# One unused 32-byte tile ahead of the phase tiles of a hybrid decoder layer

## What is computed

```python
h = _rmsnorm(x, norm_g[l])
proj = jnp.einsum('bsd,de->bse', h, w_in[l])             # 2048 -> 5456 columns
xa, ga, q, ckv, gb, qi, ki, wi = jnp.split(proj, IN_SPLITS, axis=-1)
ya = _rglru_branch(xa, ...) * jax.nn.silu(ga)            # conv, two gates of 128x128 blocks, a scan over the tokens
yb = _dsa_branch(q, ckv, qi, ki, wi, ...) * jax.nn.silu(gb)
# _dsa_branch: 16 index heads score every causal key, each query keeps 256 keys,
# 8 heads of attention over the kept latents (256 wide), read-out and value projection
y = jnp.concatenate([ya, yb], axis=-1)
x = x + jnp.einsum('bse,ed->bsd', y, w_out[l])
return _rmsnorm(x, final_norm_g)
```

## Time and profile before

| | |
|---|---|
| median of 3 runs | 1666.22 us (1665.55 to 1667.6) |
| the profiled execution's own time | 1666.16 us |
| its span, first to last instruction | 1664.4 us |
| PE busy | 1611.6 us, 97% |
| PEld busy | 1311.7 us, 79% |
| DVE, ACT, POOL busy | 51%, 35%, 25% |
| granted TensorE clock, mean | 0.994 of full |

### The profile page before, as it was taken

How to read it: one execution, slowest core, us unless ns; L and a number is a source line. 1 busy time by engine, 2 the same in 40 slices (tenths; PEclk the granted TensorE clock), 3 DMA queues, 4 the chain that set the end, 5 groups by cost and what they waited for, 6 DMA issues and landing times.

```text
span 1664.4 us, 21182 instructions
## 1 busy us (share of the span) xinstructions
PE 1611.6 (97%) x7403; PEld 1311.7 (79%) x7403; DVE 856.6 (51%) x1497; ACT 580.3 (35%) x849; POOL 421.7 (25%) x285
## 2 busy tenths in 40 slices
PE   4999999999999999999999999999998899999998
PEld 4678999888888888888888888777776788888886
DVE  7317555577777777865555554377777000031003
ACT  7225555433443343332111111354555122232320
POOL 1112222222222221222222222210010444444550
PEclk8999999999999999999999999999999999999999
DMA  7412111122222122223222221321222532237322
GB/s 258 88 39 67 48 44 38 32 54 60 60 59 61 38 54 66 66 83 95 75 70 70 74 69 57 108 80 63 66 76 87 205 101 89 95 101 285 127 88 101
DMA packets 132301, 141.35 MB, mean 85 GB/s; under 512 B 8510, under 2 KB 103840, under 8 KB 129952
## 3 DMA queue, kind: packets, MB, share of 16 engines
q1 hardware_dynamic: 130720, 136.55, 26.2%
q0 software_dynamic: 1536, 4.20, 0.8%
HBM read 116.08 MB, written 24.64 MB: 85 GB/s over the span
## 4 chain that ended last, share of the span: by engine, by line
PE 84%; issue 8%; DVE 4%; ACT 2%; DMA 1%; DVEq 0%; POOL 0%; SPq 0%; ACTq 0%; POOLq 0%
PE ps L1022 17%; PE ps L1023 17%; PE ps L1024 17%; PE ps L1282 6%; PE ps L1283 6%; PE ps L1284 6%; PE ps L1109 2%; PE ps L1223 2%; PE ps L1111 2%; PE ps L1187 2%; PE ps L1200 1%; PE ps L1307 1%; PE ps L1308 1%; PE ps L1309 1%; DVE ps L1525 1%
## 5 line engine op out<-in xcount | busy, mean ns | idle before, releaser
L1022 PE MATMUL ps<-hT_hi,w_lo 128*128 128x512 f32 (+2 forms) x1376 | 531.0, 386 | 2.0 <-POOL w_lo L642 2.0
L1024 PE MATMUL ps<-hT_hi,w_hi 128*128 128x512 f32 (+2 forms) x1376 | 528.9, 384 | 0.0
L1023 PE MATMUL ps<-hT_lo,w_hi 128*128 128x512 f32 (+2 forms) x1376 | 528.8, 384 | 0.0
L642 POOL TENSOR_TENSOR w_lo<-w_raw,w_hi 128x512 fp32r<-128x512 f32 (+1 forms) x172 | 237.5, 1385 | 803.0 <-ACT w_hi L723 802.9
L1022 PEld LDWEIGHTS ps<-hT_hi,w_lo 128*128 128x128 f32 (+1 forms) x1376 | 257.0, 187 | 56.7 <-issue 3.5
L1023 PEld LDWEIGHTS ps<-hT_lo,w_hi 128*128 128x128 f32 (+1 forms) x1376 | 256.9, 187 | 53.2 <-issue 0.4
L1024 PEld LDWEIGHTS ps<-hT_hi,w_hi 128*128 128x128 f32 (+1 forms) x1376 | 256.8, 187 | 52.4 <-issue 0.2
L723 ACT ACTIVATE w_hi<-w_raw 128x512 fp32r<-128x512 f32 (+1 forms) x172 | 106.4, 627 | 524.1 <-PE ps L1024 502.8
L1282 PE MATMUL ps<-wo_hi,hT_lo 128*128 128x512 f32 x448 | 178.0, 397 | 3.1 <-DVE hT_lo L1550 3.1
L1609 DVE TENSOR_TENSOR res<-ps,res 128x512 f32<-128x512 f32 x32 | 21.8, 690 | 304.7 <-PE ps L1284 253.9
L1283 PE MATMUL ps<-wo_lo,hT_hi 128*128 128x512 f32 x448 | 177.7, 397 | 0.0
(11 more groups left out here) (179 smaller groups left out, 1712.5 us busy)
## 6 DMA issues: line engine op xcount, KB each, us to landing
w_raw<-in_w_in SPq DMA_DIRECT2D x168, 256.0 KB, 2.8
wo_raw<-in_w_out SPq DMA_DIRECT2D x64, 512.0 KB, 3.6
xin<-in_x SPq DMA_DIRECT2D x8, 1024.0 KB, 5.4
res<-in_x SPq DMA_DIRECT2D x8, 1024.0 KB, 9.4
out<-res SPq DMA_DIRECT2D x16, 512.0 KB, 3.9
y_lru_dram<-sg SPq DMA_DIRECT2D x8, 512.0 KB, 2.8
q_dram<-av SPq DMA_DIRECT2D x8, 512.0 KB, 3.7
gate_dram<-rg SPq DMA_DIRECT2D x8, 512.0 KB, 4.3
```

The costliest lines, as they stand in the source:

```text
L642: nc.gpsimd.tensor_tensor(w_lo[:, j, :, 0:n], w_raw[:, j, :, 0:n], w_hi[:, j, :, 0:n].bitcast(F32), ALU.subtract).then_inc(w_lo_s, 1)
L1022: nc.tensor.matmul(o, wlo, hi, start=(kt == 0), stop=False)
L1023: nc.tensor.matmul(o, whi, lo, start=False, stop=False)
L1024: return nc.tensor.matmul(o, whi, hi, start=False, stop=(kt == KT - 1))
```

## The change

One tile of 8 float32 (32 bytes) per partition is allocated behind `sums`, ahead of the first phase tile, in `layer`. Nothing reads or writes it. No instruction, wait or DMA is added, removed or moved. All phase tiles of all phases begin 32 bytes later, at byte 149888, which is a multiple of 64 and of 128; `hT` and the other lasting tiles stay where they are.

```diff
         w_nat = sb("w_nat", [P, QB, IH])
         sums = sb("sums", [P, QB, 3])
+        sb("line_pad", [P, 8])
 
 
         ph = ExitStack()
```

## The result

The changed kernel takes 1640.27 us (median of 4 runs, 1639.44 to 1640.71) against 1666.91 us before (4 runs). The ratio is 0.984 with a 95% interval of 0.983 to 0.986: 26.6 us less. In a later session the same kernel took 1638.54 us (5 runs, 1637.48 to 1638.66) against 1667.39 us, 0.983 (0.981 to 0.984). The forecast was 1631.4 us, its range 1627 to 1647. So the direction and the size of the gain in the main stages were right, and the two measurements lie 8.9 and 7.1 us above the forecast. The rule given for it (multiples of 64 bytes) is not the one that the runs bear out, as the experiments show.

What follows compares the result with a forecast made beforehand. TensorE, busy for 97% of the span, was taken as the bound through its matmul spacing. Gains of 21.7 + 8.9 + 2.3 + 0.4 + 1.2 + 0.3 = 34.8 us took 1666.2 to 1631.4 us; range 1627 to 1647.

Steps and rivals of the forecast that it cites:

- The rule given for it (multiples of 64 bytes): All matmuls: both operands at multiples of 64 bytes give the last output chunk's pace, 226.7 ns instead of 233.3.
- The main terms: 512-column matmuls falling from 233.3 to 226.7 ns: 21.7 us in the projection, 8.9 us in output chunks one to seven.
- (b): Rival: a rhythm between weight loads and moving stream leaves aligned matmuls at 229 to 230 ns; around 1648 us, chance 0.09.
- (c): Rival: the last chunk's operands sharing a tile, or their distance, sets its pace; no gain, 1666 us, chance 0.05.
- Rival (a): Only one operand matters, so only projection or only output gains; 1640 or 1656 us, chance 0.10, half each.
- the term of 2.3 us for 384 columns: Projection: all 768 matmuls with 384 columns gain 3 ns each, 2.3 us, bounds 0 and 5.1.
- 1.2 for scores and gates: Scores fall 3.3 ns each at 512 columns, gates to 226.7 ns; together 1.2 us.
- 0.3 forecast: Attention: 96 keys matmuls gain up to 0.6 us, half of it counted as PE waits there: 0.3 us.
- Lines of 16 bytes: Skill's SBUF rule, set against the forecast: a 32-byte shift changes no operand's place in its line; gain 0, 1666 us.
- (d): Rival: data and weights equally placed in their lines make loads hold up the stream; slower, 1697 us, chance 0.04.

Runs made afterwards that it cites:

- pad96: Changed kernel with the unused tile 96 bytes instead of 32, so phase tiles start 64 bytes past a multiple of 128: 1665.09 us, 0.999 of before.
- all_off: Changed kernel plus 32 unused bytes ahead of `hT`, so every matmul operand lies 32 past a multiple of 64: 1637.93 us, 0.983 of before.
- w_only: Kernel before with `w_*` moved by 32 bytes and what follows by 64; output tiles stay 32 past a multiple of 64: 1647.23 us, 0.990.
- after_again: The changed kernel itself, run again in a later session: 1638.54 us, 0.983 of the kernel before.
- ht_off: Kernel before with 32 unused bytes ahead of `hT` instead of behind `sums`; phase tiles at multiples of 64: 1669.09 us, 1.002 of before.
- sums_first: Kernel before with `sums` (96 bytes) allocated ahead of `hT` and no unused tile: 1665.77 us, 0.999 of before.
- w_off16: Changed kernel with `w_hi` and `w_lo` 16 bytes past `hT`'s place and everything behind them 64 bytes off: 1653.02 us, again 1652.74.
- ix_off: Changed kernel with `ki` and `stack` (index stage) moved 32 bytes further: 1637.91 us, 0.982 of the kernel before.

## Why the prediction was right, and where it was not

**The main terms held, for a reason that was put wrongly.** The step from 233.3 to 226.7 ns in 3264 projection and 1344 output matmuls was priced at 21.7 and 8.9 us. From the first gate matmul to the first keys matmul, a stretch with 2880 of the 3264, 19.5 us are gone, as much as the forecast's prices give for it and its gates; from the first output matmul to the last chunk 8.8. Reading the last chunk as a copy of the state after the change was sound. But it had two properties at once: its operands were at multiples of 64, and they were alike. I took the first for the cause and put the second under rivals (b) and (c). That the change meets both was luck: pad96 also puts all of them at multiples of 64, my rule would have forecast the same 1631 us for it, and it took 1665.09. The rows that speak against the first stood in my own list: the last six gate matmuls, both operands 32 off and alike, had 228.3 ns in the earlier trace rows including the step back to the projection; I read that as a middle pace. The kernel before, in the timeline of PE of that turn, has this ninth gate matmul too:

```profile
416.44 0.39 PE L1139 MATMUL ps<-xc_hi,wg_hi 128*128 128x512 f32 x1
```

The eight spacings from 414.59 us up to it have a mean of 231 ns, the four from it to 417.35 us 227.5: the gates came in slow and settled near the good pace, all at 32 past a multiple of 64. all_off shows that alike is what matters. Rival (a), that one of the two stages has another cause, falls with the changed kernel itself: the stationary operand moved in the projection, the moving one in the output, and both stages took the good pace; in w_only each stage's pace goes with its own distance.

**The index stage gave nothing: the term of 2.3 us for 384 columns and most of the 1.2 for scores and gates.** The pace of 384 columns did fall where triples follow each other alone, from 176.7 ns to 173.3. The timeline of PE in the changed kernel, nine apart:

```profile
215.06 0.33 PE L1023 MATMUL ps<-hT_hi,w_lo 128*128 128x384 f32 x1
...
216.62 0.33 PE L1023 MATMUL ps<-hT_hi,w_lo 128*128 128x384 f32 x1
```

1.56 us by nine. But the earlier trace rows had shown both paces in the kernel before, and the faster one, 173.3 ns, where scores stand between the triples. That is most of the stage: 468 of the 768 matmuls stand in groups of six between scores and had 174.4 ns in the mean. The step that failed is the count: I gave all 768 matmuls a gain that only the unbroken runs have. From the last `c_sq` matmul to the last score, summed over the starts in both traces, the six unbroken runs of 30 gained 0.5 us and the stage's 90 projection matmuls of 512 columns 0.3. Against that the groups of six went from 174.4 to 175.2 ns each and lost 0.4, the waits behind the unbroken runs grew by 0.4, and scores of 256 columns, 117 ns and then 122 in the mean of one of their two lines, cost 0.1. The stage took 206.4 us before and 206.3 after. The first tile of 384 columns, which lies before it, gained its 0.3. The gates fell to 226.7 ns, as said.

**The granted clock took the rest.** Stretches in which the clock fell to half, in the changed kernel: length, busy time of each engine, clock, DMA share, GB/s:

```profile
68.50:71.90 3.40, 3.40 (x10) 2.63 (x9) 3.37 (x7) 2.02 (x4) 2.61 (x3) 0.50 0.72 176
...
1054.90:1058.40 3.50, 3.50 (x11) 2.69 (x11) 1.44 (x5) 0.83 (x2) 0.00 (x0) 0.51 0.01 2
1259.70:1263.20 3.50, 2.96 (x4) 1.41 (x5) 2.58 (x7) 1.51 (x3) 0.00 (x0) 0.51 0.14 32
```

The kernel before has none of these three in its profile. Between 40 and 1650 us it has only one, as the output begins, which the changed kernel has at 1280.2 us too:

```profile
1297.50:1300.90 3.40, 3.22 (x8) 2.55 (x9) 0.00 (x0) 0.00 (x0) 0.00 (x0) 0.50 0.80 241
```

At half clock 3.4 us of dense matmuls do the work of 1.7. The first stretch and a slightly slower 80-column tile turn the 2.0 us that I had for the first four tiles into a loss of 0.5; the other two fall in attention, which is 2.2 us longer: the turn of its loop with the second one took 29.8 us, its full turns else 28.2, and 28.3 before. They fall where PE has had gaps just before, in the lead-in and in attention (PE was busy for 6.0 of the 8.5 us up to 68.5, for 3.3 of the 4.9 us up to 1054.9). Which gaps are hit differs from run to run: after_again has the first and the third but not the second, and pad96, ht_off and sums_first, which are no faster than the kernel before, have such stretches too. A stretch like the third, in the last part of attention, is in 11 of the 13 traces at either pace of the projection; the kernel before and w_off16 alone lack it. Attention took 234.8 us in the profile before, the shortest of all (up to 239.9), so that profile was a lucky base to subtract from. The times show it as well: the runs of ix_off with a mean clock of 0.992, 0.993 and 0.995 took 1641.4, 1637.7 to 1638.4 and 1634.4 us. I had noted the mean clock of 0.994 and priced nothing; those five runs alone lie 7.0 us apart. Whether a faster kernel is hit more often stays open.

Put by stage, with the forecast's prices: 2.5 us are missing up to the last `c_sq` matmul (2.0 forecast, 0.5 lost), 3.4 in the index stage (3.5 forecast, 0.6 of them for its matmuls of 512 columns, 0.1 came), 2.5 in attention (0.3 forecast, 2.2 lost) and 0.2 in the output. That is the 8.6 us by which the profile's span of 1638.2 us is over 1664.4 - 34.8.

**Lines of 16 bytes.** The Trainium skill, "SBUF — State Buffer", "Specifications (TRN2)", gives 16-byte cachelines, from which I had worked out that a shift by 32 changes nothing. By that rule the time would have stayed; it fell by 26.6 us. But 16 bytes do appear: 16 short of the good distance is good, 16 past it can be, 32 is not.

**The other rivals.** (b), a rhythm, was half right: there is one, it has history, and it shows at distances other than 0 and in scores, not in the projection of the changed kernel. (c) had said that the distance might be the cause and the offset chance. It was given 0.05 as a case of no gain; its mechanism is the true one, but the change happens to make the distance right too, by 32 bytes. I had held against it that projection and output have very different distances and the same pace; modulo 256 these are -32 and +32. (d), a slower meeting of loads and data, has no row for it: with equal places the pace is the best seen.

## What to carry to other kernels

In a dense stream of float32r matmuls, read the spacing of starts over many matmuls and compare stages: 233.3 against 226.7 ns in one kernel is worth a search for what differs. Try the stationary operands at a multiple of 256 bytes from the moving ones; whether either was at a multiple of 64 by itself was of no account here. A better pace in one place of a trace has several properties at once, so vary them one at a time (here: move both operands together as in all_off, and one by another amount as in pad96) before making a rule of one; the unused 32 bytes work in this kernel because of what `hT`'s place happens to be.

## What the runs showed of the hardware

- Two settled paces of a matmul with 128 rows and 512 float32r columns and a new stationary operand each time, at the full granted clock: 226.7 and 233.3 ns, and 228.9 in one case. For 384 columns 173.3 and 176.7 ns. Other engines and DMAs showed no part in it: 233.3 ns with DVE, ACT and POOL idle, 226.7 with DVE and DMAs at work.
- The pace goes with the distance of the two operands modulo 256 bytes (0 and -16 good, +16 either, 32, 64 and 128 off bad, with 228.9 ns at -64), and at +16 and 128 also on what ran before: at +16 it went from 233.3 to 226.7 ns across 16 plain float32 transposes and stayed there for the next 304 us, twice at the same place, and at 128 from 233.3 to 232.5 ns there.
- The neighbours count too: with both of their operands at the same bytes the gates had 230.0 ns in ht_off and 226.7 in the changed kernel, where `hT` lies 32 bytes elsewhere.
- Plain float32 matmuls showed no such effect: the transposes had 109 ns before and after, though their distance changed by 32 bytes, and the read-out 216.0 ns for 256 columns in both and in w_only and w_off16, which change its distance by 32 and 64.
